# A ring of four weight chunks, refilled by two chunks per transfer instead of one

## The chip, the cores and the metric

The kernel runs on one core of a Trainium2 chip. Its engines are PE (TensorE, matrix products), ACT (ScalarE), DVE (VectorE), POOL (GpSimd) and SP (SyncE, which here only issues transfers). They run side by side, each works through its own list of instructions in order, and they meet at semaphores. The metric is the device time of one execution in microseconds (us), and the number given for a kernel is the median of several executions.

## The reference

Two blocks of a language model, one after the other, on 256 tokens of width 2048 (16 learned tokens stand ahead of them in the first block, so 272). Everything is float32.

```
first_block:  h = concat(meta_tokens, x)                       # 272 x 2048
              z = rmsnorm(h) @ w_in                            # 2048 -> 6592 columns
              mix = concat(short_conv(z[:3072]), rwkv7(z[3072:])) @ w_out
              h = h + rmsnorm(mix)
              gate, up = split(rmsnorm(h) @ w_gate_up)         # 2 x 5632 columns
              h = h + rmsnorm((silu(conv3(gate)) * up) @ w_down)
second_block: q, k, v = split(rmsnorm(h) @ w_in2)              # 32 query heads, 8 key heads of 64
              s = q k / 8 + bias[distance], window of 128 keys, one sink per head
              h = h + (softmax(s) v) @ w_out2
              gate, up = split(conv3(rmsnorm(h) @ w_up2))      # here both halves are convolved
              h = h + (silu(gate) * up) @ w_down2
```

The eight products with large weights are most of the work. They read 744 x 512 KB, some 390 MB, once.

## The kernel before

**Layout.** Features lie on the 128 partitions, tokens along the free axis. A float32 product is made of halves: a weight tile w is split into wh, its value rounded to the matrix format, and wl = w - wh, and the activations likewise into xh and xl; PE adds three products (xh wh, xl wh, xh wl). Lines L1856 (xh and xl side by side as one operand of 512 columns) and L1858, or L1860 to L1862, hold them.

**Chunks.** The weights of the eight projections stand in the order of use in 744 chunks, each 128 partitions x 2 x 512 values (512 KB): two blocks of 128 input features for four blocks of 128 output features. `PROJECTIONS` has them as groups x chunks: w_in 13 x 8, w_out 4 x 8, gate_up 22 x 8, down 4 x 22, in2 6 x 8, out2 4 x 8, up2 22 x 8, down2 4 x 22. `FIRST[name]` is a projection's first chunk (up2's is 480, down2's 656). A chunk in memory is one block, 4 KB for each partition.

**The ring.** `raw`, `wh` and `wl` have `RING` = 4 slots each, and chunk n uses slot n mod 4 of all three. Four engines pass a chunk on:

- SP asks for it (L498 for all but the first 16 chunks, that is for 728 of them). The request of chunk n waits until low_ready says that the low half of chunk n - 4 is made, since both halves read raw. Every landing adds 16 to the semaphore `landed[slot]`.
- ACT makes the high half (`high`, L586, 1.06 us): it waits for landed[slot], and for chunk_used, which says that PE is done with chunk n - 4.
- DVE makes the low half (`low`, L1042, 1.23 us) and adds 1 to low_ready. That is PE's signal for chunk n and SP's for chunk n + 4.
- PE multiplies (about 2.8 us a chunk) and adds 1 to chunk_used.

**The order of the work** is written out by hand for each engine, with the calls of `highs` and `lows` (so many high or low halves in a row) between the other work. SP and PE have only loads and products there. On ACT squares, square roots, exponentials, copies out of PE's banks and the gates stand between the high halves; on DVE norms, convolutions, the gate's product, softmax and residuals between the low ones. The places that matter below:

- End of w_out: PE's last group ends, ACT takes the squares of its four banks (L601, then L671, sq_last), and PE sums these and goes on to the norm.
- Attention (in2 to out2): score rows are made on DVE (L1720, L1722), exponentials on ACT (L955), their transposes are copied to `pt` by ACT (L965), and PE multiplies pt by the values (L2439). Products of out2's chunks are woven in (L2400 to L2402).
- First gate of up2: DVE takes the inverse `rstd` of a root (L1061), then for the first group of 4 x 128 outputs the convolution of the gate half (`gt`, `cv`), that of the value half (`ut`), the product `av`, and then low halves.
- The loop of up2 (`feed_forward("up2", True)`, `pair(p)`, 10 turns of 16 chunks, 8 for a gate group and 8 for a value group). ACT: high 12, copy `ups` of the gate group (`low_halves(p, 0)`, L901), high 13 and 14, `gated` (the silu, L890), highs 15 to 20, copy `ups` of the value group, highs 21 to 23, `activated` (L894), highs 24 to 27, all counted from the turn's start. DVE: low 12, `joined` (L1607, L1609: the two halves of the product are added and scaled) and the gate's convolution with lows 13 and 14 inside it, lows 15 to 20, `joined` and the value's convolution with lows 21 and 22 inside, the product av, low 23, `split` (L1658), lows 24 to 27. The loop of gate_up is the same without the copies, without the first join and without the convolution of the value half.
- In down2 there is nothing on ACT and DVE but halves and, at a group's end, squares and sums.

Other transfers are few: constants and h at the start, a 4 MB load `bias` before attention, gup (1 MB) in the first block, and the output at the end.

Of the kernel before, what the change touches and what calls it, by code (L numbers as in the profile page):

```python
# [59 lines left out]
RING = 4  # L60
# [85 lines left out]
def program(nc, d):  # L146
    with ExitStack() as ctx:
        def sem(name):
            return ctx.enter_context(nc.semaphore(name))
# [10 lines left out]
        def persistent(name, shape, dt=F32):  # L160
            t = at(name, shape, dt, base[0])
            size = 4 * int(np.prod(shape[1:]))
            base[0] += -(-size // 32) * 32
            return t

        raw = persistent("raw", [P, RING, 2, 512])
# [127 lines left out]
        landed = [sem(f"landed{i}") for i in range(RING)]  # L294
        high_ready, low_ready, chunk_used = sem("high_ready"), sem("low_ready"), sem("chunk_used")
# [57 lines left out]
        G0, n = {}, 0  # L353
# [9 lines left out]
        def over(ap, tiles):  # L363
# [5 lines left out]
        SUMS = [("w_in", L), ("w_out", LG), ("gate_up", LG), ("down", SEQ),  # L369
                ("in2", SEQ), ("out2", SEQ), ("up2", SEQ)]  # L370
        SUM = {name: s for s, (name, _) in enumerate(SUMS)}
        TOKENS = dict(SUMS)
        OUTPUTS = ("w_out", "down", "out2")
# [81 lines left out]
        @block.sync  # L455
        def _(sp):
            def tiles_in(j):
                sp.dma_start(h[:, 2 * j:2 * j + 2, :], d["ht"][:, 2 * j:2 * j + 2, :]).then_inc(h_landed[j], 16)

            constants = [(ones, "ones", consts), (table, "table", consts), (onehot, "onehot", consts),  # L460
                         (maskrow, "maskrow", consts), (ident, "ident", consts), (bones, "bones", consts),
                         (aup, "aup", lora_landed), (wdu, "wdu", lora_landed), (reset, "reset", lora_landed),
                         (lmask, "lmask", lora_landed), (gmask, "gmask", lora_landed), (identc, "identc", lora_landed),
                         (center, "center", lora_landed)]

            for name, groups, chunks in PROJECTIONS:
                weights = d[name]
                first = FIRST[name]
                if first == 0:
                    for j in range(RING):  # L470
                        if j == 1:
                            sp.wait_ge(h_landed[0], 16)
                        if j >= 2:
                            sp.wait_ge(landed[j - 2], 16)
                        if j == 0:
                            sp.dma_start(raw[:, 0, 0], weights[0, :, 0]).then_inc(half_landed, 16)
                            sp.dma_start(raw[:, 0, 1], weights[0, :, 1]).then_inc(landed[0], 16)
                            continue
                        sp.dma_start(raw[:, j], weights[j]).then_inc(landed[j], 16)
                        tiles_in(j)  # L480
                    later = constants
                    for n in range(RING, 4 * RING):
                        sp.wait_ge(low_ready, n - RING + 1)
                        sp.dma_start(raw[:, n % RING], weights[n]).then_inc(landed[n % RING], 16)
                        if n < 2 * RING:
                            tiles_in(n)
                            continue
                        for dst, src, sem_of in later[0:2]:
                            sp.dma_start(dst[:], d[src]).then_inc(sem_of, 16)
                        later = later[2:]  # L490
                        if n == 3 * RING - 1:
                            sp.dma_start(vec[:, KT:N_VEC], d["vec"][:, KT:N_VEC]).then_inc(vec_rest, 16)
                start = 4 if first == 0 else 0
                with sp.Fori(start, groups * chunks // RING) as i:
                    for j in range(RING):

                        sp.wait_ge(low_ready, i * RING + (first + j - RING + 1))
                        sp.dma_start(raw[:, j], weights[i * RING + j]).then_inc(landed[j], 16)  # L498

            for x, (t, f0, f1) in enumerate(OUT_PARTS):  # L500
                sp.wait_ge(out_ready, x + 1)
                sp.dma_start(d["out"][:, t, f0:f1], ft[:, t, f0:f1]).then_inc(stored, 16)
                if x in (1, 3):
                    sp.wait_ge(shared_ready, t + 1)
                    sp.dma_start(d["out"][:, t, 0:SHARED[t]], ft[:, t, 0:SHARED[t]]).then_inc(stored, 16)
            sp.wait_ge(stored, 16 * (len(OUT_PARTS) + 2))
# [68 lines left out]
        def _(act):  # L575

            def high(n, slot):

                if not isinstance(n, int):
                    act.wait_ge(landed[slot], (n - slot) * (16 // RING) + 16)  # L580
                    act.wait_ge(chunk_used, n - (RING - 1))
                else:
                    act.wait_ge(landed[slot], 16 * (n // RING + 1))
                    if n >= RING:
                        act.wait_ge(chunk_used, n - RING + 1)
                act.activation(wh[:, slot], raw[:, slot], ACT.Copy).then_inc(high_ready, 1)  # L586

            def highs(first, count, slot=0):
                if isinstance(first, int):
                    count = clamp(first, count)  # L590
                for c in range(count):
                    high(first + c, (slot + c) % RING)
# [10 lines left out]
            def take_root(name):  # L603

                act.wait_ge(ss_done, SUM[name] + 1)
                if name in OUTPUTS:
                    n = TOKENS[name]
                    b, _, m = token_parts(name)[-1]
                    act.activation(root_column[0:m, 0:b + 1], ps[0:m, 0:b + 1, 0], ACT.Sqrt, scale=1.0 / D,
                                   bias=eps[0:m, 0:1]).then_inc(root_ready, 1)  # L610
                    highs(kept(name), 1, kept(name) % RING)
                    act.wait_ge(row_again, OUTPUTS.index(name) + 1)
                    act.activation(rstd_post[:, 0:n], ps[:, 2, 0:n], ACT.Copy).then_inc(rstd_ready, 1)
                    return
                for b, col, t, n in sum_parts(name):
                    last = act.activation(root[:, t:t + n], ps[:, b, col:col + n], ACT.Sqrt, scale=1.0 / D, bias=eps[:, 0:1])
                last.then_inc(root_ready, 1)
# [176 lines left out]
            def refill(s):  # L794

                if ENDED.get(s - 2) == 9:
                    conv_high(0)
                for n in USED[s]:
                    high(n + RING, n % RING)
# [23 lines left out]
            for c in range(N_RC):  # L823
                n, t0 = CHUNK_LENGTHS[c], T0[c]
# [147 lines left out]
            for i in range(N_PAIRS + 2):  # L972
                if i >= 2:
                    out_high(i - 2)
                if i:
                    for n in WEAVE_USED[i - 1][1]:
                        high(n + RING, n % RING)
                if i < N_PAIRS:
                    softmax_pair(i)
                if 1 <= i < SHORT_PAIRS or i == N_PAIRS:  # L980
                    turn_out(i - 1)
                for n in WEAVE_USED[i][0]:
                    high(n + RING, n % RING)
# [48 lines left out]
        def _(dve):  # L1032
# [31 lines left out]
            def inverse_column_of(name):  # L1064

                dve.wait_ge(root_ready, SUM[name] + 1)
                b, _, m = token_parts(name)[-1]
                dve.reciprocal(inverse_column[0:m, 0:b + 1], root_column[0:m, 0:b + 1]).then_inc(column_ready, 1)
                dve.wait_ge(row_done, OUTPUTS.index(name) + 1)
# [1544 lines left out]
```

## Time and profile before

| | |
|---|---|
| three runs, us | 2329.53, 2330.22, 2330.49; median 2330.22 |
| the profiled execution, us | 2329.48 |
| its span, first to last instruction, us | 2327.5 |
| mean granted clock of TensorE, as a share of full speed | 0.998 |
| HBM read, MB, and mean rate over the span, GB/s | 402.74, 174 |
| high halves (L586): busy us, count, mean ns | 777.0, 743, 1057 |
| low halves (L1042): busy us, count, mean ns | 909.4, 743, 1236 |
| DVE busy, ACT busy, share of the span | 66%, 46% |

The profiled execution is 2.0 us longer than its span, and what is read from the trace is counted in the span. In a timeline a row is an instruction or several alike in a row (x2, x3): its start, its length, the engine, the line of the program, the operation with its output and inputs, and in brackets how long the engine had stood idle before it and what ended that. "<-PE ps" behind a high half means that it waited for a free slot of the ring; "<-DMA raw" would mean that it waited for the load. SPq is SP's queue in which requests stand.

### The profile page before, as it was taken

The numbers are of one execution on the slowest core, as the hardware profiler recorded it, in microseconds if no ns is written. First come the engines' busy times: TensorE is split into PE (matmuls) and PEld (weight loads), VectorE is DVE, ScalarE is ACT, GpSimd is POOL, SyncE is SP. The second block draws the span as 40 slices with busy tenths as digits, with TensorE's granted clock in tenths as the row PEclk, the third lists the DMA queues.
The fourth block names the chain that finished last, engine by engine and source line by source line (L and its number), as shares of the span: only waits on it lengthen the run. The fifth ranks groups of instructions, "written<-read, shape, count | busy, mean of one in ns | idle before, by whom it ended". The sixth has DMA issues, their size and how long they took to land.

```text
span 2327.5 us, 51071 instructions
## 1 busy us (share of the span) xinstructions
PE 2312.2 (99%) x20274; PEld 2143.8 (92%) x20274; DVE 1525.7 (66%) x1963; ACT 1068.1 (46%) x1360; POOL 116.2 (5%) x144
## 2 busy tenths in 40 slices
PE   9999999999999999999999999999999999999998
PEld 9999999999999999998889999899888888888886
DVE  5678877748666656654444866558877777774444
ACT  5543344445443444343444556655444444444443
POOL 2000000013000000000000300012000000000000
PEclk9999999999999999999999999999999999999999
DMA  7554333455655555555565474464556555556664
GB/s 252 173 160 122 112 110 120 137 194 159 195 182 186 179 187 185 181 188 184 189 189 182 153 245 128 127 198 155 181 190 193 184 191 177 191 191 198 190 187 147
DMA packets 115979, 407.00 MB, mean 175 GB/s; under 512 B 12896, under 2 KB 18112, under 8 KB 115456
## 3 DMA queue, kind: packets, MB, share of 16 engines
q1 hardware_dynamic: 110816, 396.06, 53.4%
q10 hardware_dynamic: 5024, 8.87, 1.1%
q8 instruction: 114, 1.87, 0.3%
q14 instruction: 25, 0.20, 0.0%
HBM read 402.74 MB, written 2.15 MB: 174 GB/s over the span
## 4 chain that ended last, share of the span: by engine, by line
PE 94%; DVE 4%; issue 1%; ACT 1%; DVEq 0%; POOL 0%; ACTq 0%; POOLq 0%
PE ps L1856 19%; PE ps L1860 12%; PE ps L1861 12%; PE ps L1862 12%; PE ps L1858 10%; PE ps L2501 3%; PE ps L2500 3%; PE ps L2502 3%; PE ps L2044 2%; PE ps L2034 2%; PE ps L1833 2%; PE ps L1832 2%; PE ps L1831 2%; PE ps L2035 2%; PE ps L2036 2%; PE ps L2400 1%
## 5 line engine op out<-in xcount | busy, mean ns | idle before, releaser
L1042 DVE TENSOR_TENSOR wl<-raw,wh 128x1024 fp32r<-128x1024 f32 x743 | 909.4, 1236 | 670.7 <-ACT wh L586 670.2
L586 ACT ACTIVATE wh<-raw 128x1024 fp32r<-128x1024 f32 x743 | 777.0, 1057 | 896.9 <-PE ps L1862 334.1
L1860 PE MATMUL ps<-xh,wh 128*128 128x256 f32 (+2 forms) x2048 | 581.4, 284 | 0.7 <-DVE wl L1042 0.4
L1861 PE MATMUL ps<-xl,wh 128*128 128x256 f32 (+2 forms) x2048 | 578.9, 283 | 0.0
L1862 PE MATMUL ps<-xh,wl 128*128 128x256 f32 (+2 forms) x2048 | 578.3, 282 | 0.0
L1856 PE MATMUL ps<-x,wh 128*128 128x512 f32 x1280 | 448.2, 393 | 0.8 <-DVE wl L1042 0.8
L1860 PEld LDWEIGHTS ps<-xh,wh 128*128 128x128 f32 x2048 | 385.1, 188 | 2.2 <-issue 1.4
L1861 PEld LDWEIGHTS ps<-xl,wh 128*128 128x128 f32 x2048 | 385.8, 188 | 0.2
L1862 PEld LDWEIGHTS ps<-xh,wl 128*128 128x128 f32 x2048 | 385.5, 188 | 0.0
L1858 PE MATMUL ps<-x,wl 128*128 128x256 f32 x1280 | 357.1, 279 | 0.0
L1856 PEld LDWEIGHTS ps<-x,wh 128*128 128x128 f32 x1280 | 239.8, 187 | 58.1 <-DVE wl L1042 1.1
L1858 PEld LDWEIGHTS ps<-x,wl 128*128 128x128 f32 x1280 | 239.8, 187 | 0.0
L1856 PE MATMUL ps<-act,wh 128*128 128x512 f32 x528 | 185.4, 393 | 0.0
L1858 PE MATMUL ps<-act,wl 128*128 128x256 f32 x528 | 149.3, 283 | 0.0
L2500 PE MATMUL ps<-wh,act 128*128 128x512 f32 x352 | 139.0, 395 | 0.0
L2501 PE MATMUL ps<-wl,act 128*128 128x512 f32 x352 | 138.9, 395 | 0.0
L2502 PE MATMUL ps<-wh,act 128*128 128x512 f32 x352 | 138.9, 395 | 0.0
L1856 PEld LDWEIGHTS ps<-act,wh 128*128 128x128 f32 x528 | 99.2, 188 | 22.9
L2034 PE MATMUL ps<-xh,wh 128*128 128x260 f32 x384 | 114.6, 298 | 0.8 <-DVE cg L1303 0.8
L2035 PE MATMUL ps<-xl,wh 128*128 128x260 f32 x384 | 108.2, 282 | 0.0
L2036 PE MATMUL ps<-xh,wl 128*128 128x260 f32 x384 | 108.2, 282 | 0.0
L527 POOL TENSOR_TENSOR sq_sum<-sq_sum,sq 128x256 f32<-128x256 f32 (+2 forms) x99 | 90.3, 912 | 327.8 <-ACT sq L601 319.0
(327 smaller groups left out, 3366.4 us busy)
## 6 DMA issues: line engine op xcount, KB each, us to landing
raw<-in_gate_up SPq DMA_DIRECT2D x176, 512.0 KB, 3.7
raw<-in_down SPq DMA_DIRECT2D x176, 512.0 KB, 4.2
raw<-in_up SPq DMA_DIRECT2D x176, 512.0 KB, 4.1
raw<-in_w_in SPq DMA_DIRECT2D x103, 512.0 KB, 3.8
raw<-in_in SPq DMA_DIRECT2D x48, 512.0 KB, 3.7
raw<-in_w_out SPq DMA_DIRECT2D x32, 512.0 KB, 4.2
raw<-in_out SPq DMA_DIRECT2D x32, 512.0 KB, 3.6
bias<-bias_rows ACTq DMA_DIRECT2D x1, 4096.0 KB, 25.8
```

What stands on the lines that cost most here:

```text
L586: act.activation(wh[:, slot], raw[:, slot], ACT.Copy).then_inc(high_ready, 1)
L1042: dve.tensor_tensor(wl[:, slot], raw[:, slot], wh[:, slot].bitcast(F32), ALU.subtract).then_inc(low_ready, 1)
L1856: pe.matmul(ps[:, 4 * parity + m, :], w_high, hi.rearrange("p s n -> p (s n)"), start=(k == 0), stop=False)
L1858: last = pe.matmul(out, w_low, hi[:, 0], start=False, stop=(k == 2 * per - 1))
L1860: pe.matmul(out, w_high, hi, start=(k == 0), stop=False)
L1861: pe.matmul(out, w_high, lo, start=False, stop=False)
L1862: last = pe.matmul(out, w_low, hi, start=False, stop=(k == 2 * per - 1))
L2034: pe.matmul(out, w_high, hi, start=(k == 0), stop=False)
L2035: pe.matmul(out, w_high, lo, start=False, stop=False)
L2500: pe.matmul(out, acth[:, k, tokens], wh[:, slot, kk, :], start=(k == 0), stop=False)
L2501: pe.matmul(out, acth[:, k, tokens], wl[:, slot, kk, :], start=False, stop=False)
L2502: last = pe.matmul(out, actl[:, k, tokens], wh[:, slot, kk, :], start=False, stop=(k == 2 * per - 1))
```

## The change

SP's loop at L498 takes two chunks per request: 1 MB into the neighbouring slots j and j + 1 (j = 0 or 2), asked for when the low half of the chunk four before the *second* one is made (the constant goes from first + j - 3 to first + j - 2). In memory two chunks stand one behind the other; the request's pattern has the partition outermost and then the two chunks, 4 KB each. Its landing adds 16 to landed[j] alone, so that ACT waits for landed[0] for the chunks of slots 0 and 1 and for landed[2] for those of slots 2 and 3. The first 16 chunks are loaded as before. The counts of all projections are multiples of four, so pairs never straddle two of them.

```diff
--- before.py
+++ after.py
@@ -492,10 +492,11 @@
                             sp.dma_start(vec[:, KT:N_VEC], d["vec"][:, KT:N_VEC]).then_inc(vec_rest, 16)
                 start = 4 if first == 0 else 0
                 with sp.Fori(start, groups * chunks // RING) as i:
-                    for j in range(RING):
-
-                        sp.wait_ge(low_ready, i * RING + (first + j - RING + 1))
-                        sp.dma_start(raw[:, j], weights[i * RING + j]).then_inc(landed[j], 16)
+                    for j in range(0, RING, 2):
+
+                        sp.wait_ge(low_ready, i * RING + (first + j - RING + 2))
+                        sp.dma_start(raw[:, j:j + 2], weights[bass.ds(i * RING + j, 2)].rearrange("c p a b -> p c a b")).then_inc(
+                            landed[j], 16)
 
             for x, (t, f0, f1) in enumerate(OUT_PARTS):
                 sp.wait_ge(out_ready, x + 1)
@@ -577,10 +578,10 @@
             def high(n, slot):
 
                 if not isinstance(n, int):
-                    act.wait_ge(landed[slot], (n - slot) * (16 // RING) + 16)
+                    act.wait_ge(landed[slot // 2 * 2], (n - slot) * (16 // RING) + 16)
                     act.wait_ge(chunk_used, n - (RING - 1))
                 else:
-                    act.wait_ge(landed[slot], 16 * (n // RING + 1))
+                    act.wait_ge(landed[slot if n < 4 * RING else slot // 2 * 2], 16 * (n // RING + 1))
                     if n >= RING:
                         act.wait_ge(chunk_used, n - RING + 1)
                 act.activation(wh[:, slot], raw[:, slot], ACT.Copy).then_inc(high_ready, 1)
```

The list of SP's instructions for one turn of its loop over w_out, before (an ISA row is the wait):

```order
L498 ISA [waits low_ready]
L498 DMA raw<-in_w_out 128x1024
L497 REGISTER_ALU
L498 ISA [waits low_ready]
L498 DMA raw<-in_w_out 128x1024
L497 REGISTER_ALU
L498 ISA [waits low_ready]
L498 DMA raw<-in_w_out 128x1024
L497 REGISTER_ALU
L498 ISA [waits low_ready]
L498 DMA raw<-in_w_out 128x1024
```

and after:

```order
L498 ISA [waits low_ready]
L498 DMA raw<-in_w_out 128x2x1024
L497 REGISTER_ALU
L498 ISA [waits low_ready]
L498 DMA raw<-in_w_out 128x2x1024
```

Four waits with a request each became two, with twice the data. The same holds for the loops of all eight projections. On ACT, in w_in, where the first chunks of SP's loop are used, before:

```order
L586 ACTIVATE wh<-raw 128x1024 [waits chunk_used,landed0]
L586 ACTIVATE wh<-raw 128x1024 [waits chunk_used,landed1]
L586 ACTIVATE wh<-raw 128x1024 [waits chunk_used,landed2]
L586 ACTIVATE wh<-raw 128x1024 [waits chunk_used,landed3]
L736 DMA bias_rows<-erow 32x384 [waits erow_ready]
```

and after (x2 stands for two alike in a row; L587 is L586 of before):

```order
L587 ACTIVATE wh<-raw 128x1024 [waits chunk_used,landed0] x2
L587 ACTIVATE wh<-raw 128x1024 [waits chunk_used,landed2] x2
L737 DMA bias_rows<-erow 32x384 [waits erow_ready]
```

No instruction of ACT moves; only the semaphore that the second chunk of a pair waits for is another. DVE's, PE's and POOL's lists stay as they are.

## Rows read from the trace of the kernel before

**Rows 1.** The page, busy shares (section 1) and chain (section 4).

```profile
PE 2312.2 (99%) x20274; PEld 2143.8 (92%) x20274; DVE 1525.7 (66%) x1963; ACT 1068.1 (46%) x1360; POOL 116.2 (5%) x144
...
PE 94%; DVE 4%; issue 1%; ACT 1%; DVEq 0%; POOL 0%; ACTq 0%; POOLq 0%
```

**Rows 2.** The waits of PE on low halves: us, times, longest.

```profile
PE ps L1856 <- DVE wl L1042: 0.8, 1, 0.8
...
PE ps L1860 <- DVE wl L1042: 0.7, 2, 0.4
```

**Rows 3.** The page, section 3, queue of the loads: packets, MB, share.

```profile
q1 hardware_dynamic: 110816, 396.06, 53.4%
```

**Rows 4.** Requests at L498: end of down2, a turn of up2, down2.

```profile
DMA to landing us min/median/max: 3.3/3.5/3.6
...
DMA to landing us min/median/max: 3.4/3.8/4.9
...
DMA to landing us min/median/max: 4.2/4.2/4.5
```

**Rows 5.** Windows, last columns clock, DMA share, GB/s, during the bias load.

```profile
1350.00:1355.00 5.00, 5.00 (x45) 5.00 (x44) 3.36 (x3) 1.69 (x2) 0.00 (x0) 1.00 1.05 385
```

**Rows 6.** Timelines of DVE, SP, ACT in down2: start, us, engine, operation.

```profile
2150.06 1.23 DVE L1042 TENSOR_TENSOR wl<-raw,wh 128x1024 fp32r<-128x1024 f32 x1 [1.57 <-ACT wh L586]
...
2151.46 0.33 SPq L498 DMA_DIRECT2D raw<-in_down  x1
...
2160.12 1.06 ACT L586 ACTIVATE wh<-raw 128x1024 fp32r<-128x1024 f32 x1 [1.73 <-PE ps L2502]
```

**Rows 7.** End of w_out: L498's request at 527.6; timeline of ACT.

```profile
DMA to landing us min/median/max: 6.5/6.5/6.5
...
532.39 1.06 ACT L586 ACTIVATE wh<-raw 128x1024 fp32r<-128x1024 f32 x1 [1.86 <-PE ps L1833]
...
535.22 0.39 ACT L671 ACTIVATE sq_last<-ps 128x258 f32<-128x258 f32 x1 [0.33 <-PE ps L1833]
```

**Rows 8.** Start of attention: timelines of SP, DVE, ACT, PE.

```profile
1373.14 0.33 SPq L498 DMA_DIRECT2D raw<-in_in  x1
...
1377.60 1.22 DVE L1042 TENSOR_TENSOR wl<-raw,wh 128x1024 fp32r<-128x1024 f32 x1
...
1381.98 0.79 ACT L965 ACTIVATE pt<-ps 128x768 f32<-128x768 f32 x1
...
1383.42 0.88 PE L2439 MATMUL ps<-pt,vt 128*64 128x128 f32 x12
```

**Rows 9.** First gate of up2: timelines of SP and DVE; the chain.

```profile
1609.58 0.33 SPq L498 DMA_DIRECT2D raw<-in_up  x1
...
1615.80 1.75 DVE L1061 RECIPROCAL rstd<-root 128x256 f32<-128x256 f32 x1 [1.45 <-ACT root L616]
...
1640.28 1.15 DVE wl L1042
```

**Rows 10.** First turn of up2's loop: timelines of DVE and ACT.

```profile
1642.97 3.49 DVE L1042 TENSOR_TENSOR wl<-raw,wh 128x1024 fp32r<-128x1024 f32 x3
...
1661.59 3.50 DVE L1042 TENSOR_TENSOR wl<-raw,wh 128x1024 fp32r<-128x1024 f32 x3 [2.07 <-ACT wh L586]
...
1648.04 1.06 ACT L586 ACTIVATE wh<-raw 128x1024 fp32r<-128x1024 f32 x1 [0.27 <-DMA raw<-in_up]
...
1667.04 1.06 ACT L586 ACTIVATE wh<-raw 128x1024 fp32r<-128x1024 f32 x1 [1.80 <-PE ps L1858]
```

**Rows 11.** A later turn of up2's loop: timeline of DVE.

```profile
1693.27 1.23 DVE L1042 TENSOR_TENSOR wl<-raw,wh 128x1024 fp32r<-128x1024 f32 x1 [1.51 <-ACT wh L586]
...
1705.72 3.50 DVE L1042 TENSOR_TENSOR wl<-raw,wh 128x1024 fp32r<-128x1024 f32 x3 [2.07 <-ACT wh L586]
...
1715.67 1.23 DVE L1042 TENSOR_TENSOR wl<-raw,wh 128x1024 fp32r<-128x1024 f32 x1 [1.51 <-ACT wh L586]
...
1729.96 2.35 DVE L1042 TENSOR_TENSOR wl<-raw,wh 128x1024 fp32r<-128x1024 f32 x2
```

## The prediction

> **What bounds the kernel now.** I read the busy shares and the chain first: TensorE (PE) is busy 99% of the span and holds 94% of the chain [rows 1]. Then the waits of PE: none names a load, and those on low halves (wl), through which a late load would come, are 0.8 and 0.7 us [rows 2]. The loads' queue is busy 53.4% [rows 3]. So nothing is there to gain beyond 1.5 us. What the change can do is use up the slack between a load's landing and PE. I read that slack from the timelines of ScalarE (ACT), VectorE (DVE) and SP. Times of an idle are in brackets with what ended it; "<-PE" behind a high half means that the ring of four held it, not the load.
>
> **How long one request takes.** A 512 KB request lands 3.5 us after its start where loads stand alone, 3.8 (median) in the up2 loop, 4.2 in down2 [rows 4]. With the queue saturated by a 4 MB load, 385 GB/s flow [rows 5], so 524,288 more bytes need 1.36 us, rounded 1.4. One request of 1 MB (call its time L) is in no weight row. Bounds: 3.5 us, if the second block travels beside the first; 7.0, if it costs a whole second request. I take 3.5 + 1.4 = 4.9, since the rate is measured and the rest is latency, paid once.
>
> The rate is not what is short here [rows 3]; the Trainium skill ("DMA: Bandwidth & Descriptors", section Bandwidth) advises batching to 1 MiB or more for three quarters of peak, which would change nothing where only arrival counts. The same page gives 2.0 us plus bytes over 436 GB/s, under which a second 512 KB adds 1.2 us; its table next to that has 6.15 us for 1 MB. No row decides between them; the sums by both stand at the rivals.
>
> **What changes.** 728 requests at L498 become 364. Each of the 364 saves SP 0.33 us of issuing, which is off every chain. The odd chunk of a pair is asked for when it was before and lands 1.4 us later. The even one is asked for one chunk later (2.8 to 3 us) and lands 1.4 us later on top: 4.2 us of slack lost. Behind a late high half ACT's in-order queue stands still: squares, roots, softmax and gates; behind its low half DVE's does.
>
> **Steady stages.** In down2 a low half ends at 1.23 after 2150.06 = 2151.29, its request starts at 2151.46 (0.17 later) and lands at 2155.7; the high half that reads it starts at 2160.12, held by PE [rows 4, 6]. Slack 4.5, after the change 0.3. Missing it would cost nothing yet: high and low take 2.3 us, PE wants the chunk three chunks (8.4 us) after the high half's start. Where evacuations bunch the lows, a high half comes up to 4 us late by this reckoning, still inside that 6 us. The gate_up loop lacks up2's convolution of the value half (about 4.5 us of DVE a turn), so its limit on L, derived as below, is above 6. All cost 0.
>
> **Where the cover is thin** (requests, then who waits):
> - End of w_out. The pair of 138 and 139 is asked for at 527.6, as 139 is now, and 139 took 6.5 us behind other loads [rows 7], so 534.1; with one more chunk in front of it, which takes the place of chunk 140, I keep 534.0. The high half of 532.39 starts 1.6 later, and 1.06 of it and four squares of 0.39, the last of which now ends at 535.61, follow back to back: 536.6, less 0.2 by which neighbours overlap: +0.8. PE waits for exactly these sums.
> - Attention's first pair. The request that started 1373.14 becomes the 1 MB one: landed 1378.0 [rows 8]. With 1.06 for the high half, the low half goes from 1377.60 to 1379.1; the scores behind it on DVE, the exponentials and the copy to pt shift by 1.5; pt was ready at 1381.98 + 0.79 = 1382.77, PE used it at 1383.42: 1.5 - 0.65 = +0.9.
> - First gate of up2. The chain here is DVE's from rstd (1615.80) to the low half ending at 1641.43, which PE takes at once [rows 9]. The request of 1609.58 becomes 1 MB: landed 1614.5, high half until 1615.5, low half until 1616.8, and rstd stands behind it: 1616.7. +0.9.
> - First turn of the up2 loop. The request behind that low half is asked for at 1641.43 + 0.17 + 0.9 and lands 1647.4; the next starts at the end of the second of the three lows from 1642.97 (1645.3 + 0.9 + 0.2 = 1646.4) and lands 1651.3. The high half of 1648.04 starts 3.3 late; the copy ups behind it on ACT, the join on DVE, the convolution, the gate, and so the low half of 1661.59 follow by 3.3 [rows 10]: it ends 1666.1. PE begins that chunk at 1664.1 (the high half of 1667.04 is released by its end, 2.8 later), plus the 0.9 it is already behind: +1.1.
>
> **The up2 loop itself** is the term that decides. One turn is 16 chunks of 2.80 us (1693.27 to 1715.67 are 8, paced by PE), 44.8 us [rows 11]. After the change a closed path runs through it: from the low half at 1693.27 over join and convolution to that of 1705.72, 12.45; the three lows there, 3.50; request 0.17; L; high half 1.1; from the low half at 1715.67 with no wait for a load through join, convolution, product and split to the end of the two lows of 1729.96, 16.64; again 0.17, L and 1.1. That is 35.13 + 2 L. It fits into 44.8 up to L = 4.83. At 4.9 it is 44.9. On top the pair asked for 2.3 us earlier needs 2.8 of data, so the first L grows by 0.5: +0.6 a turn. At L = 4.7 it is +0.1. I take 0.35 over the nine remaining turns: +3.2.
>
> **Sum.** 0.8 + 0.9 + 0.9 + 1.1 + 3.2 = 6.9 us, rounded 7, on the profiled execution of 2329.5 (span 2327.5 and 2.0 around it): 2336.5. The median of the runs stands 0.7 above that execution, so 2337. Ends: with L = 3.5 every term is 0 (the first gate's low half would end 1615.4, before 1615.80), and the 1.5 us of waits on wl are all that could be won: 2329. With L = 5.6 a turn grows by 35.1 + 11.2 + 1.2 - 44.8 = 2.7.
>
> **Rivals.**
> - The cover holds. L is 4.7 or less; the skill's formula, taken as the difference of two sizes, gives 3.5 + 1.2 = 4.7. The turn fits, and what is left are the four single places, each 0.2 to 0.3 smaller: +3, 2333, not told from no change. For it: the limit is 4.83, the lone row goes down to 3.3, and a turn's slack was not exhausted before. Against: medians in that very loop are 3.8, not 3.5. 0.35.
> - The up2 turn is overrun. From L = 5.2 on, each 0.1 us costs 0.2 a turn. With L = 5.6: 9 x 2.7 = 24 and 7 for the single places, +31: 2361. For it: landings of 4.2 in down2 and up to 4.9 in the loop at half the size [rows 4]. Against: those overlap with a neighbour, and the doubled request has fewer neighbours. With L = 7.0 it is some +75, 2405. Working with the skill's 6.15 us, a turn grows by about 4, or 2370 to 2375. Together 0.17.
> - Loads run better and PE's small waits shrink: at most 1.5 us, 2328.7. Lone, since no wait on a load is on the chain; with what I don't see 0.04.
> - The change doesn't do what it says: a request whose outermost dimension were the two blocks would use two of the 16 DMA engines. At 24 GB/s an engine (385 / 16) 1 MB takes 22 us, 364 times: 8000 us more. The order has 128x2x1024, partitions outermost, so 0.01.
>
> **Chances and range.** My forecast, +5 to +12, has 0.43. About 0.2% (4.7 us) is what a measurement of this kernel tells from no change. Slower by more: 0.43 less a sliver, and the overrun, 0.59. Within: the holding cover, 0.37. Faster: 0.04. The range goes from 2331.5, inside the rival with cover, to 2352 (L of about 5.3); for the forecast alone it is 2335 to 2342.
>
> **What would show it.** Requests of raw at 1024 KB, 364 of them, median to landing 4.9 (forecast), 4.7 or less (cover), 5.2 or more (overrun). ACT's waits for raw grow from some tens of us at most to hundreds, in total. PE gets waits on wl at the end of each up2 turn, 0.1 to 0.6 us each, about ten; the rest of the span in the stages gate_up, down and down2 stays as it is. At 1383 PE waits for pt about 0.9 us; rstd in up2 starts 0.9 later against PE's chunk before it. The forecast is wrong if up2's loop shows no wait on wl, or waits above 1.2 us a turn, or if gate_up, down or down2 grow.

## The result, and the profile after

The changed kernel takes 2354.76 us (median of four runs, 2351.93 to 2355.70), the kernel before beside it 2330.35. The ratio is 1.0105, with a 95% interval of 1.0093 to 1.0117: slower by 24 us. The sign was forecast, the size was not: +7 was said, and 2354.8 lies outside the stated range. The profiled execution took 2351.93 with a span of 2350.1, which is 22.6 more than the span before.

The page of the changed kernel: shares, chain, queue of the loads, and the requests of `raw` in up2 and down with their median time to landing.

```profile
PE 2319.7 (99%) x20274; PEld 2146.5 (91%) x20274; DVE 1521.0 (65%) x1963; ACT 1060.3 (45%) x1360; POOL 116.3 (5%) x144
...
PE 63%; DVE 13%; issue 10%; DMA 9%; ACT 3%; POOL 1%; DVEq 1%; SPq 0%; ACTq 0%; POOLq 0%
...
q1 hardware_dynamic: 104992, 396.04, 48.8%
...
raw<-in_down SPq DMA_DIRECT2D x88, 1024.0 KB, 4.9
raw<-in_up SPq DMA_DIRECT2D x88, 1024.0 KB, 4.9
```

Loads, which were nowhere on the chain before, are 9% of it, and PE fell from 94% to 63% [rows 1]. The 1 MB request lands in 4.9 us, as forecast from the lone request's 3.5 and the rate of the saturated queue [rows 4, 5]. The Trainium skill ("DMA: Bandwidth & Descriptors", section "Anatomy of one DMA — SWDGE (gpsimd) path") gives 2.0 us plus bytes over 436 GB/s, for transfers that GpSimd issues; these stand in SP's queue. By that a second 512 KB adds an estimated 1.2 us, where the profile shows 1.4 over the lone request. The 6.15 us for 1 MB in the table of its section Bandwidth, also for GpSimd, was not seen as a median here. The queue is less busy than before (48.8% against 53.4% [rows 3]): moving the bytes was never short.

Where the time went is best seen from the start of PE's first product of a chunk, against the same chunk before (each from PE's first chunk on). A second execution of the same program was profiled later (`pairs_again`, 2360.21 us).

| stretch (chunks) | forecast, us | profile | second profile |
|---|---|---|---|
| start and w_in (0 to 103) | 0 | 1.4 | 0.8 |
| w_out and opening of gate_up (104 to 151) | 0.8 | 7.3 | 9.0 |
| gate_up's loop, down (152 to 399) | 0 | 0.0 | 0.0 |
| in2, attention (400 to 475) | 0.9 | 2.5 | 2.6 |
| end of out2, opening of up2 (476 to 491) | 0 | 2.4 | 2.8 |
| first gate, first turn of up2 (492 to 523) | 2.0 | 2.4 | 2.8 |
| the other nine turns (524 to 667) | 3.2 | 7.0 | 12.2 |
| rest of down2 | 0 | 0.0 | 0.0 |
| sum | 6.9 | 23.0 | 30.2 |

How far a row moves by chance can be seen in the later kernels. Six of their executions have the requests of the kernel before up to the opening of gate_up; in them the first row reads 0.4 to 1.2 us, and the second 0.0 or -0.7 to -0.8. The latter three are those in which the clock did not fall at the opening of gate_up, as it did in the profile before. So the 1.4 and 0.8 us of w_in are not told from nothing.

### The group ends of w_out

The timelines of DVE, SP, ACT and PE in the changed kernel around the end of a group of w_out (start, length, engine, line; in brackets the idle time and what ended it):

```profile
490.07 3.50 DVE L1043 TENSOR_TENSOR wl<-raw,wh 128x1024 fp32r<-128x1024 f32 x3 [5.05 <-ACT wh L587]
...
491.47 0.37 SPq L498 DMA_DIRECT2D raw<-in_w_out  x1
...
496.40 1.06 ACT L587 ACTIVATE wh<-raw 128x1024 fp32r<-128x1024 f32 x1 [4.47 <-DMA raw<-in_w_out]
...
497.50 1.23 DVE L1043 TENSOR_TENSOR wl<-raw,wh 128x1024 fp32r<-128x1024 f32 x1 [3.93 <-ACT wh L587]
498.64 1.23 DVE L1543 COPY mix<-ps 128x1032 f32<-128x1032 f32 x1
...
502.58 1.72 ACT L684 ACTIVATE mix<-mix,vec 128x258 f32<-128x258 f32 x4
504.21 2.94 ACT L587 ACTIVATE wh<-raw 128x1024 fp32r<-128x1024 f32 x3
...
504.24 0.28 PE L1863 MATMUL ps<-yrh,wl 128*128 128x258 f32 x1
506.56 0.39 PE L1861 MATMUL ps<-yrh,wh 128*128 128x258 f32 x1 [2.05 <-DVE wl L1043]
```

The pair is chunks 124 and 125. In the kernel before, chunk 124 was asked for behind the low half of 120, at 483.00 (timeline of SP, below). Now it is asked for behind that of 121, and between these two low halves stand the group's copy on DVE and, on ACT, four squares and four scalings: 8.5 us later in the trace, 7.4 without the 1.1 us that everything is behind by then, not 2.8. Its high half waits 4.47 us for the load; the copy `mix`, the squares and the three high halves from 504.21 stand behind it in order, and PE stops for 2.05 us. This happened at one of w_out's three inner group ends in this profile and at two in the second. The same piece before:

```profile
481.59 1.23 DVE L1042 TENSOR_TENSOR wl<-raw,wh 128x1024 fp32r<-128x1024 f32 x1 [1.64 <-ACT wh L586]
482.74 1.23 DVE L1542 COPY mix<-ps 128x1032 f32<-128x1032 f32 x1
489.00 3.50 DVE L1042 TENSOR_TENSOR wl<-raw,wh 128x1024 fp32r<-128x1024 f32 x3 [5.04 <-ACT wh L586]
...
483.00 0.33 SPq L498 DMA_DIRECT2D raw<-in_w_out  x1
```

Behind the stop comes a second loss. Windows of the changed kernel (busy times, then the granted clock, DMA share and GB/s):

```profile
502.00:506.00 4.00, 2.52 (x21) 2.31 (x20) 0.72 (x1) 3.84 (x7) 1.59 (x3) 1.00 0.01 2
506.00:510.00 4.00, 3.44 (x17) 3.44 (x18) 2.77 (x3) 1.15 (x2) 0.00 (x0) 0.63 0.55 159
...
546.00:550.00 4.00, 4.00 (x20) 4.00 (x20) 3.24 (x6) 1.80 (x5) 1.30 (x2) 0.50 0.00 0
```

PE is busy again, but the clock is at the lower level (1.2 GHz) for some 3.5 us, with 17 products in a window that holds 36 at full clock: (1 - 0.63) x 4 = 1.5 us, and 0.2 more in the next window (0.95). At the opening of gate_up the clock fell before the change too, once; now it is low there for twice as long. In windows of 4 to 5 us the time lost to the clock between 500 and 560 us is 1.7 before and 5.1 after: 3.4 of the 22.6 us. The second loss need not follow. In pairs_again PE stopped even longer at the same place, and the clock stayed at 1.00:

```profile
507.25 0.38 PE L1861 MATMUL ps<-yrh,wh 128*128 128x258 f32 x1 [2.41 <-DVE wl L1043]
...
507.00:511.00 4.00, 3.75 (x31) 3.75 (x32) 2.47 (x3) 0.84 (x1) 0.00 (x0) 1.00 0.61 190
```

### A turn of up2

Timelines of DVE and ACT, one turn of the loop in the changed kernel:

```profile
1756.63 1.23 DVE L1043 TENSOR_TENSOR wl<-raw,wh 128x1024 fp32r<-128x1024 f32 x1 [1.66 <-ACT wh L587]
...
1769.07 3.50 DVE L1043 TENSOR_TENSOR wl<-raw,wh 128x1024 fp32r<-128x1024 f32 x3 [2.07 <-ACT wh L587]
...
1779.08 1.23 DVE L1043 TENSOR_TENSOR wl<-raw,wh 128x1024 fp32r<-128x1024 f32 x1 [0.18 <-ACT wh L587]
...
1793.36 2.35 DVE L1043 TENSOR_TENSOR wl<-raw,wh 128x1024 fp32r<-128x1024 f32 x2
...
1801.91 1.22 DVE L1043 TENSOR_TENSOR wl<-raw,wh 128x1024 fp32r<-128x1024 f32 x1 [1.48 <-ACT wh L587]
...
1775.44 2.01 ACT L587 ACTIVATE wh<-raw 128x1024 fp32r<-128x1024 f32 x2 [4.51 <-DMA raw<-in_up]
1777.98 1.06 ACT L587 ACTIVATE wh<-raw 128x1024 fp32r<-128x1024 f32 x1 [0.53 <-DMA raw<-in_up]
...
1800.82 1.06 ACT L587 ACTIVATE wh<-raw 128x1024 fp32r<-128x1024 f32 x1 [1.83 <-DMA raw<-in_up]
```

This is the closed path of the forecast, piece by piece [rows 11]: 12.44 from the first low half to the three, 3.50 for them, 5.41 to the high half of 1777.98, 1.10, 16.63 to the end of the two low halves, 5.11 to the next high half, 1.09. That makes 45.28 us where PE alone needs 44.80. Each wait for a load is 0.17 (request), the time to landing (5.1 and 4.8 in this turn), and 0.10 from the landing to the high half, which the forecast left out.

The waits of PE and of ACT in the changed kernel (us in total, times, longest):

```profile
PE ps L1857 <- DVE wl L1043: 7.0, 12, 1.3
PE ps L1861 <- DVE wl L1043: 3.8, 5, 2.0
PE ps L1881 <- ACT sq_last L672: 1.8, 2, 1.2
...
ACT wh L587 <- DMA raw<-in_up: 152.0, 63, 5.3
...
ACT wh L587 <- DMA raw<-in_down: 47.1, 17, 4.6
ACT wh L587 <- DMA raw<-in_gate_up: 45.8, 18, 4.6
ACT wh L587 <- DMA raw<-in_w_out: 23.7, 7, 7.0
```

PE's waits on wl are 10.8 us against 1.5 [rows 2]; ten of those at L1857 are the ends of up2's turns. ACT waits 47.1 and 45.8 us for loads in down with down2 and in gate_up, and PE loses nothing there: a wait alone says little, what stands behind it decides.

### The profile page after: what moved, and what is told of

Same layout as the page of the kernel before. It is cut to its first block, busy times and chain, and to the rows that moved or that the text cites. A ratio compares the mean times of both kernels' runs of the same rounds, so it can differ in the third digit from the quotient of the medians.

```text
span 2350.1 us, 49615 instructions
## 1 busy us (share of the span) xinstructions
PE 2319.7 (99%) x20274; PEld 2146.5 (91%) x20274; DVE 1521.0 (65%) x1963; ACT 1060.3 (45%) x1360; POOL 116.3 (5%) x144
## 3 DMA queue, kind: packets, MB, share of 16 engines
q1 hardware_dynamic: 104992, 396.04, 48.8%
## 4 chain that ended last, share of the span: by engine, by line
PE 63%; DVE 13%; issue 10%; DMA 9%; ACT 3%; POOL 1%; DVEq 1%; SPq 0%; ACTq 0%; POOLq 0%
PE ps L1861 9%; PE ps L1862 9%; PE ps L1863 9%; PE ps L1857 7%; DMA raw<-in_up 6%; DVE wl L1043 5%; PE ps L2502 3%; PE ps L2503 3%; PE ps L2501 3%; PE ps L1859 3%; ACT wh L587 2%; PE ps L2045 1%; PE ps L2035 1%; DVE ut L1590 1%; PE ps L1834 1%
## 5 line engine op out<-in xcount | busy, mean ns | idle before, releaser
L587 ACT ACTIVATE wh<-raw 128x1024 fp32r<-128x1024 f32 x743 | 771.0, 1055 | 924.5 <-PE ps L1863 263.1
L1857 PE MATMUL ps<-x,wh 128*128 128x512 f32 x1280 | 450.1, 394 | 7.0 <-DVE wl L1043 7.0
L1857 PEld LDWEIGHTS ps<-x,wh 128*128 128x128 f32 x1280 | 239.8, 187 | 67.8 <-DVE wl L1043 11.1
L1857 PE MATMUL ps<-act,wh 128*128 128x512 f32 x528 | 185.4, 393 | 0.0
L1857 PEld LDWEIGHTS ps<-act,wh 128*128 128x128 f32 x528 | 99.2, 188 | 22.9
```

Of the source, the lines that this page charges most:

```text
L1857: pe.matmul(ps[:, 4 * parity + m, :], w_high, hi.rearrange("p s n -> p (s n)"), start=(k == 0), stop=False)
```

## The experiments

Theory A: a pair costs where its request path has less room than it takes, in two ways: its even chunk is asked for late by the distance of the two low halves (lateness), and it lands 1.4 us later (size). Rivals: size alone (B), lateness alone (C), a cost per pair anywhere (D).

**late_singles**: two 512 KB requests, both at the pair's time.

```diff
                     for j in range(RING):
-                        sp.wait_ge(low_ready, i * RING + (first + j - RING + 1))
+                        if j % 2 == 0:
+                            sp.wait_ge(low_ready, i * RING + (first + j - RING + 2))
                         sp.dma_start(raw[:, j], weights[i * RING + j]).then_inc(landed[j], 16)
```

> Two requests of 512 KB instead of one of 1 MB, both asked for at the pair's time (when the second slot's low half is made). Theory A (lateness and size both cost: the even chunk of a pair is asked for late by however long ACT's and DVE's other work stands between the two low halves, up to 8 us at the group ends of w_out, and 1 MB lands 1.1 to 1.4 us later): the up2 loop is back at 44.8 us a turn, since its path has room up to a time to landing of 4.83 us; at the group ends of w_out and the opening of gate_up part of the 7.3 us lost there stays. In all +2 to +6 us over the kernel before. Rival B (only the size of the request costs): within 1 us of the kernel before. Rival C (only the lateness costs, the size nothing): like the changed kernel, +24.

Measured: 2334.00 against 2329.85, ratio 1.0016 (1.0006 to 1.0025), +4.2. The loop of up2 loses 0.1 us in all; w_out and the opening of gate_up lose 3.5 where the changed kernel lost 7.3. Half of that is again the clock, low in two windows where it was low in one:

```profile
540.00:544.00 4.00, 4.00 (x22) 4.00 (x21) 2.10 (x5) 2.09 (x6) 0.29 (x1) 0.54 0.01 2
544.00:548.00 4.00, 4.00 (x24) 4.00 (x24) 3.74 (x5) 1.74 (x6) 1.42 (x3) 0.61 0.00 0
```

B and C, as put there (under 1 and +24), both fall: lateness alone costs at w_out, and most of the 24 us needs the size on top.

**middle_pairs**: per four slots one single, a pair in slots 1 and 2, one single.

```diff
-                    for j in range(0, RING, 2):
-                        sp.wait_ge(low_ready, i * RING + (first + j - RING + 2))
+                    for j, count in ((0, 1), (1, 2), (3, 1)):
+                        sp.wait_ge(low_ready, i * RING + (first + j + count - RING))
```

> Per four slots one 512 KB request (slot 0), one 1 MB request for slots 1 and 2, one of 512 KB (slot 3): half of the weights come in pairs, and the two low halves that such a pair follows never have an evacuation or join between them at the places that lost time (at w_out's group ends the block stands between slots 0 and 1, in up2 behind slot 0). Theory A: lateness at most one chunk and a convolution step (2.8 us), so w_out and gate_up's opening lose nothing or under 1 us, the up2 loop under 0.3 us a turn: +0 to +5 in all. Rival B (size costs, lateness not): half of the loss, +12.

Measured: 2335.05, ratio 1.0022 (1.0013 to 1.0032), +5.2, just above A's range and far below B's 12. w_out's group ends and the turns of up2 lose nothing; 3.1 us are lost in w_in and 1.9 around the opening of gate_up, places that this alignment meets otherwise. It is the alignment of a pair to the work between the low halves that counts, not how much comes in pairs.

**up2_pairs, steady_pairs, first_pairs**: pairs in a range of chunks, singles elsewhere (the odd slots' semaphores then count fewer landings).

```diff
+PAIRED = [(480, 744)]          # up2_pairs; steady_pairs: [(152, 404)]; first_pairs: [(16, 480)]
...
+                cuts = sorted({start, end} | {(x - first) // RING for r in PAIRED for x in r if start < (x - first) // RING < end})
+                for lo, hi in zip(cuts, cuts[1:]):
+                    with sp.Fori(lo, hi) as i:
```

> Pairs in up2 and down2 alone (chunks 480 to 743), single requests before. Theory A: the loss in up2's opening and first turns (1.5 and 2.2 us) and its nine later turns (0.8 us each) comes back and down2 costs nothing: +9 to +13. If a stage's loss depended on the stages before it (a shared delay, not one of its own), it would be under +5.

> Pairs in gate_up from its 17th chunk on and in down (and in the first four chunks of in2), chunks 152 to 403, single requests elsewhere: 126 of the 364 pairs. Theory A: these stages have more slack than the pair takes away, so within 1 us of the kernel before. Rival D (every 1 MB request costs PE a little, 24 us over 364 of them): +8.

> The complement of up2_pairs: pairs for chunks 16 to 479 (w_in to out2), single requests in up2 and down2. If the losses belong to places, the profile of the changed kernel has them at 12 us before up2 begins (3.8 at w_out's group ends, 3.5 at the opening of gate_up, 0.9 and 1.4 around attention, the rest in w_in and at the end of out2): +10 to +13. If the 24 us of the changed kernel are the sum of this kernel's and the 18 us of up2_pairs, it must be +6.

Measured: up2_pairs 2348.26, ratio 1.0076 (1.0059 to 1.0093), +18.4, above the 9 to 13 expected. steady_pairs 2330.35, ratio 1.0001 (0.9991 to 1.0010): 126 pairs for nothing, D falls. PE's waits on low halves in steady_pairs are those of before [rows 2], while ACT waits 42.1 us for gate_up's loads:

```profile
PE ps L1880 <- DVE wl L1066: 0.8, 1, 0.8
...
PE ps L1884 <- DVE wl L1066: 0.7, 2, 0.4
...
ACT wh L608 <- DMA raw<-in_gate_up: 42.1, 14, 4.5
```

first_pairs 2343.80, ratio 1.0059 (1.0042 to 1.0076), +13.5, a little above the 10 to 13 expected and far from 6 (its profile has 10.8). The two halves add up to 31.9 in medians and 30.3 in profiles, where the changed kernel's profile has 23.0 and its second one 30.2. So the sum holds only against the second, and what varied had to be found.

**pairs_again, up2_again**: the same programs, profiled once more.

> The changed kernel once more, for a second profile. In an up2 turn the pair that is asked for 2.3 us behind its neighbour (chunks 4 and 5 of a turn) took 5.3 us to land in the changed kernel's profile and 6.1 in that of up2_pairs, the one before the next first join 4.9 and 5.0. Theory A: whatever these two are here, a turn is 35.4 us plus their sum (within 0.2).

> up2_pairs once more, for a second profile. If the 6.1 us of the deciding landing belongs to the kernel, it returns; if it belongs to the execution, it lies anywhere between 5.2 and 6.5, and the turn with it by the same sum.

Measured: 2360.21 and 2345.77 us (one run each). Over nine turns of up2 (chunks 508 to 651), with the mean times to landing of the two pairs on the path, read from the trace:

| kernel | landing, pair before the join of the gate | landing, pair asked for 2.3 us behind its neighbour | 35.35 + both | turn measured |
|---|---|---|---|---|
| changed | 4.91 | 5.35 | 45.61 | 45.64 |
| pairs_again | 5.12 | 5.74 | 46.21 | 46.27 |
| up2_pairs | 5.06 | 6.12 | 46.53 | 46.49 |
| up2_again | 5.10 | 5.63 | 46.08 | 46.08 |
| up2_two (below) | 5.14 | 5.27 | 45.76 | 45.73 |
| not_w_out (below) | 5.19 | 5.80 | 46.34 | 46.32 |
| not_w_out_again (below) | 5.07 | 6.21 | 46.63 | 46.59 |

One constant (35.13 in the forecast plus twice the 0.10 between landing and high half, 35.33; 35.35 fits best) fits seven executions within 0.06 us. What varies is the time to landing of one request, the one with a neighbour in flight: 5.13 to 6.91 us from turn to turn in up2_pairs. Why its last part comes late in some turns is not known. One rival was not tried: the executions ran on several chips. The two on chip 7 (up2_pairs, not_w_out_again) have 6.12 and 6.21, the two on chip 1 (pairs_again, up2_again) 5.74 and 5.63, though up2_pairs and up2_again are one program; for the changed kernel's first profile the chip is not on record. The chip can't be all, since four executions of up2_pairs on one chip still differ by 3.6 us.

**up2_mixed and up2_two**: in up2, chunks 4 and 5 of every eight (both deciding landings of a turn) singly and the rest in pairs, and the reverse.

```diff
+                        for x, count in ((0, 2), (2, 2), (4, 1), (5, 1), (6, 2)):          # up2_mixed
+                        for x, count in ((0, 1), (1, 1), (2, 1), (3, 1), (4, 2), (6, 1), (7, 1)):   # up2_two
+                            sp.wait_ge(low_ready, i * 8 + (first + x + count - RING))
```

> up2_pairs with two of the eight pairs of an up2 turn (chunks 4 and 5 of every eight, whose landings are the two on the closed path low half, join, convolution, low half) asked for singly, each at its own low half; the other six stay pairs, and so do 656 to 743 but for the first 16. Theory A (the turn is 35.4 us plus these two times to landing): they fall from 4.9 and 5.3 to 6.1 to at most 4.7, and the even one is asked for one low half sooner, so the turn has room and the nine turns cost nothing; the opening's 1.5 to 2 us stay: +0 to +4. Rival: every pair costs, so three quarters of the 18 us stay, +14.

> The reverse of up2_mixed: in up2 (and down2's first 16 chunks) only chunks 4 and 5 of every eight come as a pair, the other six singly, and everything else singly as before: 24 pairs in the whole kernel. Theory A (a turn is 35.4 us plus the times to landing of just these two pairs): with 4.9 and 5.3 to 6.1 a turn is 45.6 to 46.5 instead of 44.8, so nine turns cost 7 to 15 us, about what all 88 pairs of up2 cost: +7 to +16. Rival (cost in proportion to the number of pairs): 24 of 132 pairs, +3.

Measured: up2_mixed 2334.42, ratio 1.0018 (1.0008 to 1.0027), +4.1, just above the 4 expected, and its turns from chunk 524 on lose 0.0, with 66 pairs in up2. Its single requests of chunk 4 of a turn did not land sooner, as expected (at most 4.7), but after 5.3 us on average; the turn fits because the request is made 1.1 us sooner. up2_two 2339.94, ratio 1.0044 (1.0027 to 1.0061), +10.2 with 22 pairs in up2 and 2 in down2, 0.93 us a turn. The waits of PE and ACT from 1660 to 2090 us in up2_mixed, then PE's in up2_two:

```profile
PE ps L1884 <- DVE wl L1070: 0.4, 1, 0.4
...
ACT wh L614 <- DMA raw<-in_up: 108.2, 31, 5.3
```

```profile
PE ps L1884 <- DVE wl L1070: 6.6, 10, 1.3
```

ACT waits 108 us for loads in up2_mixed's loop and PE 0.4: three quarters of the loop's pairs are free, and the two on the closed path carry its whole loss.

**not_w_out, not_w_out_again, free_pairs**: ranges as above. not_w_out is the changed kernel with singles in 104 to 151. free_pairs has pairs in 152 to 403, up2_mixed's pattern in 496 to 671, and pairs in 672 to 743.

```diff
+PAIRED = [(16, 104), (152, 744)]                                                            # not_w_out
+                parts = [(16, 152, 1), (152, 404, 2), (404, 496, 1), (496, 672, 8), (672, 744, 2)]   # free_pairs
```

> The changed kernel with single requests in w_out and in the first 16 chunks of gate_up (104 to 151), where the profiles of pairs show 7.3 to 9 us lost at w_out's group ends and gate_up's opening. If that loss belongs to these requests it is gone: +16 to +21 over the kernel before instead of +24 to +30. If it only moved to the next thin place, it stays at +24 or more.

> not_w_out once more, for a second profile. Its first had 1.2 us at the opening of gate_up, as expected, but lost 6.4 us at the opening of up2, where the changed kernel's two profiles lost 2.4 and 2.8. If the larger loss comes from this kernel's earlier stages, it returns; if it is a matter of a few tenths of us in two landings and of whether the clock then falls, it lies between 2 and 6.5.

> Pairs only where the profiles show no cost: chunks 152 to 403 (gate_up but for its opening, down), six of eight chunks in up2 from 496 on, and 672 to 743 (down2): 228 pairs in place of 456 single requests, everything else single as before. Theory A: the cost belongs to the places, so 228 of the 364 pairs are nearly free: 0 to +3 over the kernel before, what remains coming from up2's first gate (up to 2 us in up2_mixed). Rival (cost by the number of pairs): +15.

Measured: not_w_out 2356.22, ratio 1.0116 (1.0099 to 1.0133), +26.5: the total expected of it (16 to 21) is refuted. Its profile has the place right: from chunk 104 to 152 it loses nothing (-0.7 us). The excess lies elsewhere. The nine turns of up2 cost 13.5 us, and 16.3 in the repeat (2358.47), where the changed kernel's profiles have 7.0 and 12.2: that is the landing in the table above. And from 476 to 492 it loses 5.9 us, in its repeat 6.3, where the changed kernel's two profiles lose 2.4 and 2.8 with the same requests. The timelines of PE at the first product of the sum of squares, in the changed kernel and in not_w_out, and the windows of not_w_out behind it (third number from the end: the granted clock):

```profile
1581.04 0.24 PE L1881 MATMUL ps<-ones,sq_last 128*128 128x1 f32 x1 [0.63 <-ACT sq_last L672]
```

```profile
1576.10 0.24 PE L1903 MATMUL ps<-ones,sq_last 128*128 128x1 f32 x1 [1.65 <-ACT sq_last L693]
```

```profile
1576.00:1580.00 4.00, 3.12 (x18) 3.07 (x19) 2.13 (x6) 1.29 (x3) 1.70 (x2) 0.71 0.63 242
1580.00:1584.00 4.00, 4.00 (x20) 4.00 (x20) 2.35 (x6) 1.94 (x6) 0.52 (x1) 0.50 0.00 0
```

The request of chunks 482 and 483 took 6.1 and 6.7 us there, 5.1 and 5.2 in the changed kernel. So PE stood for 1.65 us instead of 0.63, and behind the longer stop the clock fell (0.29 x 4 + 0.50 x 4 = 3.2 us in these windows), behind the shorter it didn't. The late landing is not peculiar to not_w_out: this request took 6.0 to 6.6 us in up2_pairs, up2_again and up2_mixed too. Nor does the length of the stop settle the clock: it fell in up2_again behind stops of 0.49 and 0.78 us here and stayed at 1.00 in pairs_again behind 0.78 and 0.78. Why these landings differ between two programs with the same requests at this place stays open: it returned in the repeat, so it is not chance alone, and no run isolates it.

free_pairs: 2331.59, ratio 1.0007 (0.9998 to 1.0017), +1.9, an interval that includes no change: 228 of the 364 pairs cost together about 2 us, and under 4 by the upper end of the interval. Its profile has 1.8 us in the first gate and first turn of up2, and nothing in any other stretch that has pairs.

## Why the prediction was wrong

- **Right:** the 4.9 us to landing, the steady stages at no cost (gate_up's loop, down and down2 at 0.0, against which ACT's long waits speak only in appearance), attention, first gate and first turn as thin places (2.5 + 2.4 us against 0.9 + 2.0), the sign, and the closed path of up2 with its two landings.
- **The step that failed:** "The even one is asked for one chunk later (2.8 to 3 us)". That holds where low halves follow each other chunk by chunk. At w_out's group ends 7.4 us lie between the two low halves, because the group's copy, squares and scalings stand between them. There the high half of the even chunk holds up this same block, and PE waits for it. I looked at the last request of w_out alone and gave the stretch 0.8 us; it was 7.3 and 9.0 (in the first profile 3.8 at the inner group end and 3.5 at that last place and the opening of gate_up). late_singles shows the lateness (3.5 us without the size), middle_pairs that another alignment takes it away, not_w_out that it belongs to these requests. The same shape at the end of out2 (2.4 us) was missed with it: in the kernel before, the two requests that become that pair start at 1551.00 and 1558.76.
- **A cost that was missing:** a stop of PE was priced at its length. Behind stops of 1.65 to 2.05 us the lower clock cost 1.7 to 3.2 us more, behind one of 2.41 nothing; in the changed kernel's profile it is 3.4 of 22.6.
- **A place that was mis-sized:** attention. The forecast had a stop of 0.9 us for pt; it was 1.3, and a stop of 0.7 for the low half of chunk 420 was not on the list. Its pair was asked for during the load of `bias` and took 8.8 us to land.
- **A term that was mis-sized:** the up2 turn. With 4.9, the second landing's extra 0.5 and 35.13 the working gave +0.6 a turn; I then took 0.35, a mean with the case in which the turn fits. It measured 0.84 and 1.47. In the first profile the two landings came to 10.3 us, as the working has them (4.9 and 5.4); short were the 0.25 taken off by that mean and 0.2 a turn between landing and high half. In the second they came to 10.9. The kernel before had the sign already: in its turns single requests in that place, with a neighbour in flight, took 4.7 and 5.0 us on average, and those without one 3.5. On a closed path that is longer than PE's own time every landing counts in full, so the mean of that one request is the number, not a median over all. The case with L = 4.7 was entered with +0.1 a turn; with the same extra 0.5 it is +0.2, and with L = 5.6 the extra is put at 1.2 without its working.
- **The range:** its upper end assumed up to 5.3 us for both landings, and held no room for a thin place that was not on the list.

## What to carry to other kernels

Before two transfers are merged, measure in the timeline how far apart the two events lie that free their buffers: the first transfer becomes late by that distance, and it is largest where a block of other work stands between them, which is where the slack is smallest too. Then look for closed paths through the load (buffer freed, request, landing, conversion, the same buffer freed): the merged transfer must fit with its mean time, neighbour in flight included. Where neither applies merging costs nothing, and where the bottleneck engine is 99% busy it brings nothing either: of 364 merged requests 228 could stay at +1.9 us, and no mixture that was run beats the kernel before.

## What was not expected of the hardware

- A 1 MB request that starts 2.3 us behind another took between 5.1 and 6.9 us to land in one profile (up2_pairs), where the others of a turn had means of 4.9 to 5.1. Seven executions had means of 5.3 to 6.2 for it.
- Behind a stop of TensorE of 0.63 us the granted clock stayed at 1.00; behind stops of 1.65 and 2.05 us it was 0.50 for about 3.5 us and more, and 128x258 products took 0.42 us each instead of 0.28. Behind a stop of 2.41 us (pairs_again) it stayed at 1.00, and so it did behind ten stops of up to 1.3 us in up2. The length of one stop alone does not decide: in late_singles it fell behind two stops of 0.32 and 0.75 us that only short sums of squares parted. What does was not tried.
